# A two-block transformer kernel on one Trainium2 core: value products in column halves, branch products in rounded parts, value products moved to the end of each step

## The reference

```
x = x + retention(rmsnorm(x)) @ a_w_out                      # 4 heads, chunks of 128 rows
x = x + swa(rmsnorm(x))                                      # second layer, below
    q, gate = split(h @ w_in);  q = rmsnorm(q)               # 16 query heads of 64, 2 key heads
    p = softmax over the own and the previous block of 128 keys, with bias, mask and a sink
    o = (p @ v) * silu(gate);   out = o @ w_out
y = branches(rmsnorm(x)); x = x + rmsnorm(y)                 # third layer, below
    fox:  8 heads of 64, causal softmax with a forget bias,   ya = (p @ v) * silu(za)
    diff: 4 heads, p = softmax1 - lam * softmax2, v of 128,   yb = rmsnorm(p @ v) * silu(zb)
    merged = sigmoid(ga) * (ya @ w_branch[0]) + sigmoid(gb) * (yb @ w_branch[1])
    y = merged @ w_out
```

## Time and profile before

| | |
|---|---|
| median of 3 runs | 2540.91 us (2538.79 to 2541.54) |
| the profiled execution | 2541.13 us, span 2539.4 us |
| PE | busy 2381.5 us, 94% of the span |
| PE's weight loads | 1893.9 us, 75% |
| DVE | 1032.1 us, 41% |
| ACT | 790.2 us, 31% |
| POOL | 242.5 us, 10% |
| mean granted TensorE clock | 0.973 of full speed |

### The profile page before, as it was taken

One profiled execution on the slowest core, in us unless ns is written; L12 is line 12 of the kernel. 1 busy time (PEld: TensorE's weight loads), 2 busy tenths in 40 slices (PEclk: granted clock), 3 DMA queues, 4 the chain that ended last, 5 costly groups with the idle time before them and its releaser, 6 DMA issues. The chain is left out here.

```text
span 2539.4 us, 33090 instructions
## 1 busy us (share of the span) xinstructions
PE 2381.5 (94%) x11738; PEld 1893.9 (75%) x11738; DVE 1032.1 (41%) x2938; ACT 790.2 (31%) x2088; POOL 242.5 (10%) x377
## 2 busy tenths in 40 slices
PE   6999999999979987999989799999999996999998
PEld 5867868778758876788877677777677674788877
DVE  4323223133232223545442336766766766101132
ACT  4121221221221123444442234444534443211132
POOL 0010010010100001212110000010000100100013
PEclk9999999999989998999999899999999998999999
DMA  3111111111153221011135310111001100311122
GB/s 135 45 41 61 57 41 60 41 58 35 49 193 122 103 96 50 11 49 47 48 111 153 132 51 7 58 41 53 28 25 59 40 7 8 132 35 50 50 87 88
DMA packets 94096, 162.47 MB, mean 64 GB/s; under 512 B 7096, under 2 KB 40952, under 8 KB 92416
## 3 DMA queue, kind: packets, MB, share of 16 engines
q1 hardware_dynamic: 87888, 144.81, 16.9%
q10 hardware_dynamic: 5200, 9.55, 1.0%
q0 software_dynamic: 864, 6.29, 0.7%
HBM read 131.21 MB, written 29.42 MB: 63 GB/s over the span
## 5 line engine op out<-in xcount | busy, mean ns | idle before, releaser
L91 PE MATMUL heads_p_ps<-ret_w_second_hi_sb,ret_hT_hi_sb 128*128 128x512 f32 x384 | 161.6, 421 | 0.0
L91 PE MATMUL heads_p_ps<-ret_w_second_lo_sb,ret_hT_hi_sb 128*128 128x512 f32 x384 | 149.9, 390 | 0.0
L91 PE MATMUL heads_p_ps<-ret_w_second_hi_sb,ret_hT_lo_sb 128*128 128x512 f32 x384 | 149.4, 389 | 0.0
L2551 DVE TENSOR_TENSOR mrg_sig_sb<-mrg_b_ps,mrg_sig_sb 128x512 f32<-128x512 f32 x32 | 22.1, 690 | 236.4 <-PE mrg_b_ps L2407 236.4
L2407 PE MATMUL mrg_b_ps<-mrg_w_br_sb,mrg_yT_sb 128*128 128x256 f32 x512 | 115.5, 379 | 0.0
L91 PE MATMUL att_proj_ps<-br_w_second_hi_sb,br_hT_hi_sb 128*128 128x512 f32 x256 | 110.5, 432 | 0.0
L2407 PEld LDWEIGHTS mrg_b_ps<-mrg_w_br_sb,mrg_yT_sb 128*128 128x128 f32 x512 | 96.6, 190 | 13.6
L2019 ACT ACTIVATE br_x_sb<-br_x_sb,att_max_neg_sb 128x256 f32<-128x256 f32 (+7 forms) x128 | 97.8, 767 | 23.3 <-DVE att_max_neg_sb L2226 23.3
L91 PE MATMUL att_proj_ps<-br_w_second_lo_sb,br_hT_hi_sb 128*128 128x512 f32 x256 | 100.6, 393 | 0.0
L91 PE MATMUL att_proj_ps<-br_w_second_hi_sb,br_hT_lo_sb 128*128 128x512 f32 x256 | 100.3, 392 | 0.0
L566 DVE SCALAR_TENSOR_TENSOR heads_state_sb<-heads_state_sb,heads_tab_sb,heads_kv_ps 128x512 f32<-128x512 f32 x48 | 33.8, 746 | 161.0 <-PE heads_o_ps L392 161.0
(11 more groups left out here) (430 smaller groups left out, 6167.3 us busy)
## 6 DMA issues: line engine op xcount, KB each, us to landing
early_w_kv_sb<-a_w_blocks SPq DMA_DIRECT2D x28, 1024.0 KB, 5.3
all_w_block_sb<-w_turns SPq DMA_DIRECT2D x12, 2048.0 KB, 9.7
ret_o_dram<-early_x_rows_sb ACTq DMA_DIRECT2D x32, 256.0 KB, 2.4
all_w_block_sb<-swa_turns SPq DMA_DIRECT2D x4, 2048.0 KB, 9.7
ret_out_o_rows_sb<-ret_o_dram POOLq DMA_DIRECT2D x6, 1024.0 KB, 5.4
x_dram<-early_x_rows_sb SPq DMA_DIRECT2D x12, 512.0 KB, 3.0
heads_v_sb<-x SPq DMA_DIRECT2D x8, 512.0 KB, 4.5
all_w_block_sb<-a_w_blocks SPq DMA_DIRECT2D x2, 2048.0 KB
```

The costliest lines, as they stand in the source:

```text
L91: mm = pe.matmul(out, rows[a], w[b], start=(k == 0 and a + b == 0), stop=(k == KT - 1 and b == 1))
L2551: dve.tensor_tensor(sig[:, t % 2, :], p_br[t % 2][:], sig[:, t % 2, :], ALU.mult).then_inc(prod_done, 1)
```

## The change

Three layers of edits, none in the retention layer.

- Window layer. v is now the stationary operand (128x64) and 256 columns of the transposed probabilities move; the two heads of a pair write to the upper and the lower 64 partitions of the result (`p_o[SWA_HD * a:...]`), which therefore comes out transposed. The gate is scaled by the reciprocal sums on POOL and transposed on PE instead of the output (`gate_scaled`, `gT`), and DVE multiplies product and gate (`gate_out`). The order of a step: scores, 9 products, transposes of probabilities, 9 products, query transposes, 3 products, gate transposes, 3 products, values; then the next step's scores.
- Attention. The fox value products in the same way (64 columns of v stationary, 128 columns of probabilities moving, halves above each other), z scaled and transposed before (`scale_gate`, `transpose_gate`, `copy_gate`), one multiplication after. silu from Tanh, in one DVE instruction. The query and key transposes after 18 of the 24 projection products, the values last.
- Merge. Branch outputs and branch weights are split into fp32r parts by ACT and DVE and multiplied in three products. Outputs are loaded again in each chunk, tile by tile, with two buffers; the weights' raw copy lies in x. The chunk loop is written out. Half of the gate weights have two places and are split earlier. The final g_post and y_n lie in w_raw, so g_post is loaded later.

```diff
@@ window_layer, tensor @@
-                for head in range(QUAD):
-                    for half in range(first, 2):
-                        mm = pe.matmul(p_o[:, head * SWA_HD:(head + 1) * SWA_HD],
-                                       pT[:, n % 2, head // 2, ((head % 2) * 2 + half) * P:((head % 2) * 2 + half + 1) * P],
-                                       v_all[:, t - 1 + half, g * SWA_HD:(g + 1) * SWA_HD],
-                                       start=(half == first), stop=(half == 1))
+                for half in range(first, 2):
+                    for a in range(2):
+                        cols = slice((a * 2 + half) * P, (a * 2 + half + 1) * P)
+                        mm = pe.matmul(p_o[SWA_HD * a:SWA_HD * (a + 1), 0:2 * P], v_all[:, t - 1 + half, g * SWA_HD:(g + 1) * SWA_HD],
+                                       pT[:, n % 2, :, cols], start=(half == first), stop=(half == 1))
...
                 along(range(3, 6))
+                if n <= ITEMS:
+                    transpose_queries(n - 1)
+                along(range(6, 7))
+                if 3 <= n < ITEMS + 3:
+                    transpose_gate(n - 3)
+                along(range(7, KT))
                 if 3 <= n < ITEMS + 3:
                     values(n - 3)
-                if n <= ITEMS:
-                    transpose_queries(n - 1)
-                if n >= 4:
-                    transpose_out(n - 4)
-                along(range(6, KT))
@@ attend, tensor @@
+                    if turn.fox:
+                        pe.wait_ge(zT_done, turn.number(TILES, t + 1))
                         for j in range(t + 1):
-                            mm = pe.matmul(p_o[:, cols], pT[:, a, j, :], vz[turn.fox][:, j, cols], start=(j == 0), stop=(j == t))
+                            for a in range(2):
+                                half = slice(HD * a, HD * (a + 1))
+                                mm = pe.matmul(p_o[half, 0:P], vz[True][:, j, half], pT[:, a, j, :], start=(j == 0), stop=(j == t))
...
+                    if last and last[0].fox:
+                        transpose_gate(*last)
                     if last:
                         transpose_probs(*last, 4)
                     if following:
-                        project(following, t, range(4, 7))
+                        project(following, t, range(4, 6))
+                        if projected(turn, following, t):
+                            if last:
+                                at_least(pe, sems_cp[0], bank_count(*last, 0, SEQ))
+                            transpose_qk(*projected(turn, following, t))
+                        project(following, t, range(6, KT))
...
                     if last:
                         values(*last)
@@ attend, scalar and vector @@
-                    act.activation(z_e[:], vz[turn.fox][:, t, P:2 * P], ACT.Exp, scale=-1.0).then_inc(ze_done, 1)
+                    act.activation(z_e[:], vz[turn.fox][:, t, P:2 * P], ACT.Tanh, scale=0.5).then_inc(ze_done, 1)
...
-                    dve.tensor_scalar(z_e[:], z_e[:], 1.0, None, ALU.add).then_inc(zu_done, 1)
-                    dve.reciprocal(z_e[:], z_e[:]).then_inc(zr_done, 1)
-                    dve.tensor_tensor(z_silu[:, t % 2, :], vz[turn.fox][:, t, P:2 * P], z_e[:], ALU.mult).then_inc(sz_done, 1)
+                    dve.scalar_tensor_tensor(z_silu[:, t % 2, :], z_e[:], 1.0, vz[turn.fox][:, t, P:2 * P],
+                                             ALU.add, ALU.mult).then_inc(sz_done, 1)
@@ merge @@
+            def load_rows(c, t):
+                at_least(sp, y_lo, c.times(TILES, t + 1 - RAWS))
+                sp.dma_start(y_raw[:, t % RAWS], yT_dram.rearrange("k p n -> p k n")[:, :, t * P:(t + 1) * P]).then_inc(y_in[t % RAWS], 16)
...
+            sp.wait_ge(wo_lo, 2 * KT)
+            sp.wait_ge(wo_hi, 2 * KT)
             sp.dma_start(g_post, dram["g_post_2"].broadcast_to([P, DIM])).then_inc(g_in, 16)
...
-                        mm = pe.matmul(p_br[b][:, n * QW:(n + 1) * QW], yT[:, n * PAIRS + k, t * P:(t + 1) * P], w_br[:, n * PAIRS + k, :],
-                                       start=(k == 0), stop=(k == PAIRS - 1))
+                        rows, w = ([part[:, n * PAIRS + k, :] for part in parts] for parts in (y_parts[b], w_br))
+                        for i, j in ((0, 0), (1, 0), (0, 1)):
+                            mm = pe.matmul(p_br[b][:, n * QW:(n + 1) * QW], rows[i], w[j],
+                                           start=(k + i + j == 0), stop=(k == PAIRS - 1 and j == 1))
...
+            def split_rows(c, t):
+                act.wait_ge(y_in[t % RAWS], c.times(16 * TILES // RAWS, 16 * (t // RAWS) + 16))
+                at_least(act, br_done, c.times(TILES, t - 1))
+                act.activation(y_parts[t % 2][0][:], y_raw[:, t % RAWS], ACT.Copy).then_inc(y_hi, 1)
+            def split_branches(c):
+                act.wait_ge(wbr_in, c.times(16, 16))
+                at_least(act, br_done, c.times(TILES))
+                for n in range(2):
+                    act.activation(w_br[0][:, n * PAIRS:(n + 1) * PAIRS, :], w_br_raw[:, n * PAIRS:(n + 1) * PAIRS, :], ACT.Copy).then_inc(wbr_hi, 1)
```

More of the change, by code:

```diff
@@ L1715, in turn_sync @@
                         done, u = before
-                        sp.wait_ge(yT_done, done.tiles(u + 1))
+                        sp.wait_ge(yf_done if done.fox else yT_done, done.number(TILES, u + 1))
                         row = done.number(1, 0 if done.fox else PAIRS)
@@ L1880, in transpose_out @@
                 def transpose_out(turn, t):
[L1881 removed]
+                    pe.wait_ge(y_done, turn.number(TILES, t + 1))
                     pe.transpose(p_o[:, yT_cols], y[:], ident[:]).then_inc(yT_tr, 1)
@@ L1893, in turn_pe @@
                         first_gates(t, 0)
-                    if before:
+                    if before and not before[0].fox:
                         transpose_out(*before)
+                    if last and last[0].fox:
+                        transpose_gate(*last)
                     if last:
@@ L2034, in turn_act @@
                         copy_probs(*last, 0)
-                    if before:
+                    if before and not before[0].fox:
                         copy_out(*before)
+                    if last and last[0].fox:
+                        copy_gate(*last)
                     if t < TILES:
@@ L2183, in norm_factor, with scale_gate @@
                     dve.tensor_tensor(o_rstd[:], o_gap[:], o_pow[:, 0:1], ALU.add).then_inc(orstd_done, 1)
+                def scale_gate(t):
+                    b = t % 2
+                    dve.wait_ge(sz_done, turn.tiles(t + 1))
+                    dve.wait_ge(recip_done, turn.tiles(t + 1))
+                    for a in range(2):
+                        cols = slice(HD * a, HD * (a + 1))
+                        out = dve.tensor_scalar(z_silu[:, b, cols], z_silu[:, b, cols], p_recip[:, b, a:a + 1], None, ALU.mult)
+                    out.then_inc(zs_done, 1)
                 def out_rows(turn, t):
@@ L2261, in turn_dve @@
                         divide(t)
+                        if turn.fox:
+                            scale_gate(t)
                     if last:
@@ L2310, in in_chunks, with gate_w @@
         def in_chunks(eng, chunk):
-            chunk(Place(None, 0, 0))
-            with eng.Fori(0, CHUNKS - 2) as i:
-                chunk(Place(i, 1, 1))
-            chunk(Place(None, 0, CHUNKS - 1))
+            for c in range(CHUNKS):
+                chunk(Place(None, 0, c))
+        def gate_w(c, k):
+            return w_at(c.parity == 0, k)
         def merged_parts(t):
@@ L2340, in _ @@
-            with sp.Fori(0, CHUNKS - 2) as i:
-                c = Place(i, 1, 0)
-                sp.wait_ge(br_done, c.times(TILES, TILES))
-                sp.sem_inc(wbr_free, 1)
-                load_branches(c.plus(1))
-                sp.wait_ge(w_lo, c.times(KT, KT))
-                load_gates(c.plus(2))
-            sp.wait_ge(br_done, TILES * (CHUNKS - 1))
-            load_branches(first.plus(CHUNKS - 1))
-            for half in range(2):
-                sp.wait_ge(*((w_lo, KT * (CHUNKS - 1)) if half == 0 else (wo_lo, KT)))
-                sp.dma_start(w_raw[:], w_out[:, :, half * BANK:(half + 1) * BANK]).then_inc(wo_in, 16)
@@ L2486, in chunk_act @@
                         copy_merged(c, t - 2)
+                    if t in (3, 4) and not c.is_at(CHUNKS - 1):
+                        split_gates(c.plus(1), range(2 * (t - 3), 2 * (t - 2)))
                 if not c.is_at(CHUNKS - 1):
-                    act.wait_ge(w_in_sem, c.times(16, 16))
-                    for k in range(KT):
-                        act.activation(w_at(True, k)[0], w_raw[:, k, :], ACT.Copy).then_inc(w_hi, 1)
+                    split_gates(c.plus(1), range(KT // 2, KT))
                 last = c.is_at(CHUNKS - 1)
@@ L2501, in chunk_act @@
                 copy_merged(c, TILES - 1)
+                if not last:
+                    split_branches(c.plus(1))
```

225 lines of the change are left out of this document (142 added, 83 removed).

## The result

The changed kernel took 2502.03 us (median of 4 runs, 2500.05 to 2502.42) against 2541.22 of the kernel before beside it (2538.79 to 2545.22): ratio 0.9843, 95% interval 0.9826 to 0.986. Run again on another chip it gave 0.9842 (0.9825 to 0.9859). It is faster by 39 us where 50 were forecast; the forecast's 2491 is 11 us too low, and its range, from 2477 (the low end of my case) to 2512, holds the time.

What follows compares the result with a forecast made beforehand. The prediction took the spacing of PE's instructions as the bound, except where a value comes late. Window layer -19.2, attention -15.2 and merge -15.5 summed to -49.9 us, giving 2491 us, range 2477 to 2512.

Steps and rivals of the forecast that it cites:

- my case: Whole kernel: the forecast's main case of 2491 us, own range 2477 to 2504, chance 0.68.
- Halves in pairs: Window and fox value products: column halves run two at a time; window item 1.07 us instead of 1.72.
- Rivals B and C: Value products: B, weight loads not hidden, 2535 us, chance 0.06; C, column halves one after the other, 2548, chance 0.07.
- Window layer, -19.2: Window layer: paired values save 0.65 us in each of 28 items, 0.9 in the four first tiles.
- Fox turns, -4.1 each: Attention: pairs gain 6.5 us a fox turn, less 2.4 of waits; times four, -16.4.
- The charge of 2.4 for the query transposes: Fox turns: PE waits 0.6 us for the probabilities' copy in four of eight steps; bounds 0 and 4.8.
- rival A: Attention: moved transposes and values wait more, fox +2.4 a turn, diff 1.8 instead of 0.4; 2506 us, chance 0.12.
- Diff turns, +0.4 in three turns: Attention: values come 0.9 us later, but DVE's own queue mostly holds the clamp; +1.2 us in all.
- The upper bound of 29: Diff turns: the values' full 0.9 us delay charged in 8 steps of each of four turns.
- Merge, -15.5: Merge: branch products save 0.57 us in each of 32 tiles, -18.2; three waits give 2.7 back.
- silu and tables: Attention: shorter silu on DVE counted as zero; Tanh and Exp share a table, so no reload.
- rival D: Attention: Tanh and Exp reload tables, +20 us over 32 diff steps; 2511 us, chance 0.02.

Runs made afterwards that it cites:

- win_middle: Changed kernel with the window layer's values back after 18 projection products, ahead of the query transposes; 2516.29 us, ratio 0.9922 to the kernel before.
- old_order: Changed kernel with PE's old order in the whole attention: 21 products, values, query and key transposes, 3 products; 2480.89 us, ratio 0.9769 to the kernel before.
- diff_early: Changed kernel with only the diff tiles' values back after 21 of 24 projection products, ahead of the transposes; 2492.32 us, ratio 0.9818 to the kernel before.
- the control: Changed kernel run once more, unaltered, beside some of the variants; 2498.72 us, ratio 0.9842 to the kernel before.
- att_only: Kernel before with the change's attention alone, window layer and merge as before; 2540.06 us, ratio 1.0004 to the kernel before.
- silu_old: Changed kernel with the attention's earlier silu: Exp on ACT, then add, reciprocal and multiply on DVE; 2497.09 us, ratio 0.9839 to the kernel before.
- serial: Changed kernel with all value products of one column half before the other's, in window layer and fox turns; 2516.33 us, ratio 0.992 to the kernel before.

## Why the prediction was right in sum and wrong in its parts

- **Halves in pairs: right.** 1.01 for 1.07 in the window layer. In fox turns the eight value stretches sum to 9.1 us for 9.3. Rivals B and C are refuted by 16 pairs in 1.90.
- **Window layer, -19.2: too small.** From the first scores to the last it is 24.3 us shorter. A steady step fell by 0.75 (9.86 to 9.11) instead of 0.65, the switch being 0.18 and the pairs a little faster than charged, which is 2.8. A step at a loop's end fell by 1.53 (11.29 to 9.76), 2.3 more in all than three steady ones: PE's wait of 1.2 went, and one of 0.4 for the normed queries came, which I had put at nothing. Neither wait was in the forecast. Another 3.3 were gained between the last item and the attention, and win_middle shows that this hangs on the place of the values too: there it takes 106.4 us, 105.8 before, 102.5 in the changed kernel. The last 0.8 stand ahead of the layer, where executions of one kernel differ by 1.
- **Fox turns, -4.1 each: right.** In the last one, steps 2 to 7 and the step 0 behind them sum to 73.76 before and 69.89 after, -3.9. The charge of 2.4 for the query transposes was about right: they wait 7.9 us in twelve steps, three a turn with 0.66 each where I had charged four with 0.6, and without them (old_order) the sum is 67.7, 2.2 less with its extra switches paid. So the half of rival A that speaks of the fox turns did not come.
- **Diff turns, +0.4 in three turns: the step that failed.** I wrote that the clamp "is mostly held by DVE's own queue". That holds for steps 5 to 7, where I had read it. In steps 2 to 4 the rows are short, DVE is early and the clamp waits for the values; and the values' delay doesn't end there, as ACT takes the mean square ahead of the next projection's copy. By diff_early this costs 1.7 in the turn and 0.76 in the step behind it, three times: 7.4 us instead of 1.2. The upper bound of 29 was written down and not used; rival A, which had 1.8 a turn in place of 0.4, was too low as well. Another 1.05 in the step behind is no fault of the late values. The transposed gate's wait (0.55) is half of it, a term that the forecast had not at all, and the other half is open.
- **The loop's end in the attention: not foreseen.** The scores' issue waits went from 2.9 to 5.8 in two ends, and step 7 there from 14.46 to 15.37 and from 14.70 to 15.33 where outside the loop it fell by 0.73: 3.0 us (2.3 in the control).
- **The attention's account.** Fox turns -15.3, diff turns and the step behind +10.2, loop's ends +3.0, a fall of the clock at the second loop's end +0.8, the first and the last turn and the way in +0.3, and -1.6 where a diff turn ends, which is the scatter of the clock there: -2.6, as in the table. The same account of the control gives -2.1, and in att_only, with the same work, the attention takes 1.0 longer than before. So the part is worth between nothing and 3 us, and a term under 2 us can't be read from the sum.
- **Merge, -15.5: the steady part right, the start mis-sized.** A tile takes 8.58 instead of 9.17, 0.59 for 0.57. The first wait was 3.1 for 1.6, as the transfer took 7.0 and not the median's 5.2; the half clock behind it (1.6) and a wait for the rows of tile 4 (1.9 in this execution, none in the control) were not in the sum, nor was a wait of 1.0 for the sigmoids (ACT) at the start of the second and of the third chunk. I had written that SP's queue has the rows ahead of the gates' 2 MB; in the first chunk it hasn't.
- **silu and tables: right.** ACT loads tables twice at the attention's start (1469.5 and 1481.2), as before (1497.7 and 1509.3), then none until the merge, and silu_old shows no change. (My sign of rival D, no load from 1497 us on, was put too early: the kernel before has one at 1509.3 itself.)

## What to carry to other kernels

An instruction moved on the engine that sets the time moves a whole chain: follow its result through every queue it enters, and see what stands behind the first consumer there; the price was paid two engines further on. Read the slack of a moved step in the shortest tiles as well as in the longest, since another engine is late in each. And a packing and a new order are two changes: the pairs gave here what was forecast for them, and the order around them lost it or kept it, so try the packing in the old order first. A median over several transfers hides the first, which is the one that a stage's start waits for.

## What the runs showed of the hardware

- Products on the two column halves run side by side when up to about four PE instructions of the one half stand ahead of the other's in the queue: 32 take 1.90 us in alternation, 1.95 in blocks of four, 3.26 with sixteen ahead (serial).
- A switch between column halves and the whole array costs 0.18 us (win_middle).
- The clock falls to half once where a diff turn ends: PE waits 2.4 us in its step 7 and 1.3 once or twice in the next step 0, and behind one of these its products stand 0.43 apart for a while, as at the merge's start. The granted clock is 0.50 from 1626 to 1629 us in the first execution, and there it is 1.00 in the control, which has 0.50 from 1640.5 to 1643.5. Whether that falls into step 7 or into the next step 0 differs from execution to execution (14.51 and 11.22 in one, 12.89 and 13.65 in the other, 25.7 and 26.5 in sum). So the two steps at such a boundary can be compared only as a sum, and that scatters by 0.8.
- PE's wait after the loop's jump depends on what stands around it: 1.2 to 3.1 us in the attention, up to 2.1 or none in the window layer. The cause is open.
